# Expert products dealt to the column tiles anew, and their rows turned by VectorE instead of TensorE

## The reference

```
def block_ffn(args):
    xb, e = args
    return (jax.nn.silu(xb @ w_gate[e]) * (xb @ w_up[e])) @ w_down[e]
```

## Time and profile before

| what | value |
|---|---|
| time, median of 3 runs | 1782.14 us |
| lowest and highest | 1778.94 and 1787.34 us |
| profiled execution | span 1782.2 us, the only time that its page gives |
| PE busy, PEld busy | 1547.8 us (87%), 1104.7 us (62%) |
| DVE, ACT, POOL busy | 977.4 us (55%), 649.6 us (36%), 180.4 us (10%) |
| DMA | 305.70 MB, mean 172 GB/s |
| hidden products L2647, 4992 matmuls | 309.3 us busy |
| down products L2663, 2464 matmuls | 147.3 us busy |
| transposes L2655, 77 | mean 334 ns each |

### The profile page before, as it was taken

One profiled execution on the slowest core, in us unless ns is written; L12 is line 12 of the kernel. 1 busy time (PEld: TensorE's weight loads), 2 busy tenths in 40 slices (PEclk: granted clock), 3 DMA queues, 4 the chain that ended last, 5 costly groups with the idle time before them and its releaser, 6 DMA issues. The chain is left out here.

```text
span 1782.2 us, 47179 instructions
## 1 busy us (share of the span) xinstructions
PE 1547.8 (87%) x19513; PEld 1104.7 (62%) x19513; DVE 977.4 (55%) x1789; ACT 649.6 (36%) x1646; POOL 180.4 (10%) x261
## 2 busy tenths in 40 slices
PE   5799989999978898879989788739999999996758
PEld 3588876789767888746666677625555555543323
DVE  5797743331045665569998466660404435455637
ACT  4544421112345455346667445312222222221110
POOL 0000100000045543200000000000000000000021
PEclk8899998999969999989999999859999999999879
DMA  9322315540233443130110244276467579999967
GB/s 350 118 71 90 115 45 206 177 162 7 89 116 109 127 129 97 51 127 19 42 48 7 87 154 154 80 257 244 157 225 273 199 291 370 385 396 398 382 209 299
DMA packets 150760, 305.70 MB, mean 172 GB/s; under 512 B 10670, under 2 KB 53118, under 8 KB 147202
## 3 DMA queue, kind: packets, MB, share of 16 engines
q1 hardware_dynamic: 128674, 245.33, 38.2%
q0 software_dynamic: 10336, 46.67, 7.4%
q10 hardware_dynamic: 11520, 10.49, 1.9%
HBM read 256.79 MB, written 45.66 MB: 170 GB/s over the span
## 5 line engine op out<-in xcount | busy, mean ns | idle before, releaser
L2647 PE MATMUL psum<-now_hidden,i_xm 128*32 128x256 f32 x4992 | 309.3, 389 | 28.1 <-DVE now_hidden L2753 26.3
L2647 PEld LDWEIGHTS psum<-now_hidden,i_xm 128*32 128x32 f32 x4992 | 150.3, 111 | 150.3 <-DVE now_hidden L2753 33.3
L2663 PE MATMUL psum<-now_down,i_hT 128*32 128x256 f32 x2464 | 147.3, 379 | 14.2 <-DVE now_down L2752 14.2
L2753 DVE COPY now_hidden<-raw_hidden 128x1024 f32 (+1 forms) x176 | 109.2, 692 | 78.4 <-DMA raw_hidden<-in_w_up 38.1
L2765 DVE TENSOR_TENSOR i_h<-i_silu,psum 128x128 f32<-128x128 f32 x78 | 22.2, 284 | 215.5 <-ACT i_silu L2702 215.5
L2663 PEld LDWEIGHTS psum<-now_down,i_hT 128*32 128x32 f32 x2464 | 78.8, 110 | 70.5 <-DVE now_down L2752 19.9
L1906 PE MATMUL psum<-dkT,f_qT 64*128 64x512 f32 (+1 forms) x384 | 91.2, 581 | 23.6 <-ACT f_E L1957 21.1
L2752 DVE TENSOR_TENSOR now_down<-raw_down,rep_g 128x1024 f32<-128x1024 f32 x88 | 101.8, 1218 | 8.7 <-PE psum L2663 8.7
L121 PE MATMUL psum<-hT_head,wm_head 128*128 128x512 f32 (+1 forms) x256 | 96.8, 378 | 11.2 <-DVE hT_rest L410 6.9
L1957 ACT ACTIVATE f_E<-psum,f_mx 128x1280 f32<-128x1280 f32 (+2 forms) x96 | 92.2, 968 | 16.3 <-DVE f_mx L2016 16.1
L121 PE MATMUL psum<-hT_head,wm_rest 128*128 128x512 f32 (+1 forms) x256 | 95.3, 372 | 0.0
(11 more groups left out here) (362 smaller groups left out, 3019.7 us busy)
## 6 DMA issues: line engine op xcount, KB each, us to landing
raw_hidden<-in_w_gate SPq DMA_DIRECT2D x22, 2048.0 KB, 15.5
raw_hidden<-in_w_up SPq DMA_DIRECT2D x22, 2048.0 KB, 17.1
raw_down<-in_w_down SPq DMA_DIRECT2D x22, 2048.0 KB, 11.8
wa_late<-in_w_ada POOLq DMA_DIRECT2D x16, 1024.0 KB, 6.6
yb<-i_y ACTq DMA_DIRECT2D x80, 128.0 KB
wa<-in_w_ada SPq DMA_DIRECT2D x8, 1024.0 KB, 13.7
wt<-in_w_in SPq DMA_DIRECT2D x4, 2048.0 KB, 8.4
wm<-in_w_in SPq DMA_DIRECT2D x12, 512.0 KB, 3.8
```

The costliest lines, as they stand in the source:

```text
L2647: last = nc.tensor.matmul(hidden_bank(s)[j * SUB:(j + 1) * SUB, :], xm[u][:, k, s * SUB:(s + 1) * SUB], now["hidden"][:, :, k, j * P:(j + ...
L2663: last = nc.tensor.matmul(down_bank(s)[j * SUB:(j + 1) * SUB, :], hT[s % 2][:, k * SUB:(k + 1) * SUB], now["down"][:, k, j * WIDE:(j + 1) ...
L2753: return nc.vector.tensor_copy(now[n][:, :, k, :], src)
```

## The change

The gate and up columns are dealt to the four column tiles in another way: tile j takes columns b*128 + j*32 + x for b in 0 to 3 and x in 0 to 31, where it took j*128 to j*128+127. The moving operand of a hidden product then has 8 runs of 32 columns where it had 2 runs of 128. After `mix`, block (j, b) of 32x32 in `hh` holds 32 tokens by hidden columns b*128 + j*32 and on. Turning each such block where it stands gives the same `hT` as before: chunk b, partitions 32j to 32j+31. VectorE does this with one block transpose from `hh` to `hT`, right behind the product, with a wait for that product and one for the down products that last read this `hT`. `turn_h` on TensorE and `keep_h` on ScalarE are gone, and `down` waits for VectorE's transpose. `down` also waits for the output copy of the block before the last, where it waited for that of the last.

```diff
+    def by_blocks(ap):
+        return ap.rearrange("p (w b x) -> p w b x", w=2, x=SUB)
+    def columns_of(ap, j):
+        return ap.rearrange("p w (b j x) -> p j w b x", j=SUBS, x=SUB)[:, j]
...
-                        last = nc.tensor.matmul(hidden_bank(s)[j * SUB:(j + 1) * SUB, :], xm[u][:, k, s * SUB:(s + 1) * SUB],
-                                                now["hidden"][:, :, k, j * P:(j + 1) * P], start=(k == 0), stop=(k == KD - 1),
+                        last = nc.tensor.matmul(by_blocks(hidden_bank(s)[j * SUB:(j + 1) * SUB, :]), xm[u][:, k, s * SUB:(s + 1) * SUB],
+                                                columns_of(now["hidden"][:, :, k, :], j), start=(k == 0), stop=(k == KD - 1),
                                                 tile_position=(0, j * SUB))
...
-            def turn_h(b, s):
-                pe.wait_ge(mixed, b + 1)
-                pe.wait_ge(h_kept, b)
-                nc.tensor.transpose(m.bank(4, P), hh[s % 2][:, :], ident).then_inc(h_turned, 1)
             def down(b, s, place):
-                pe.wait_ge(h_kept, b + 1)
-                pe.wait_ge(y_kept, b)
+                pe.wait_ge(h_turned, b + 1)
+                if b >= 1:
+                    pe.wait_ge(y_kept, b - 1)
                 pe.wait_ge(copied["down"], place * KE + KE)
...
                 hidden(b + 1, v, r, after, range(KD // 2))
-                turn_h(b, s)
                 hidden(b + 1, v, r, after, range(KD // 2, KD))
                 down(b, s, here)
...
-            def keep_h(b, s):
-                act.wait_ge(h_turned, b + 1)
-                nc.scalar.activation(hT[s % 2][:, :], m.bank(4, P), ACT.Copy).then_inc(h_kept, 1)
...
             def mix(b, s):
                 dve.wait_ge(silued, b + 1)
                 nc.vector.tensor_tensor(hh[s % 2][:, :], hs[:, :], hidden_bank(s)[:, P:2 * P], ALU.mult).then_inc(mixed, 1)
+                dve.wait_ge(mixed, b + 1)
+                if b >= 2:
+                    dve.wait_ge(used["down"], (b - 1) * KE)
+                nc.vector.transpose(hT[s % 2][:, :], hh[s % 2][:, :]).then_inc(h_turned, 1)
```

More of the change, by code:

```diff
@@ L2564, in experts @@
     x_kept = [m.sem(f"i_x_kept{u}") for u in U2]
-    silued, mixed, h_turned, h_kept, y_kept = (m.sem("i_" + n) for n in ("silued", "mixed", "h_turned", "h_kept", "y_kept"))
+    silued, mixed, h_turned, y_kept = (m.sem("i_" + n) for n in ("silued", "mixed", "h_turned", "y_kept"))
     ybt = d["yb"].rearrange("(q s p) (j n) -> q j p s n", s=SUBS, p=SUB, j=SUBS)
@@ L2715, in body @@
                 b = q * SUBS + s
-                keep_h(b, s)
                 if X_PARTS[s][0] < X_PARTS[s][1]:
```

## The result

The changed kernel takes 1793.25 us (median of 10 runs, 1788.90 to 1797.45), beside 1783.22 us for the kernel before on the same chip (10 runs, 1777.91 to 1789.12): a ratio of 1.0058, interval 1.0041 to 1.0074. It is slower by about 10 us where I forecast 22 us less. A time in a trace is that of one profiled execution: span 1795.6 us after, 1782.2 before. The profiled execution of the changed kernel is the slowest of its ten, so the traces differ by somewhat more than the medians.

The account below looks back on a forecast made before the run. TensorE was taken to bound the experts stage up to 1460 us, expert weight loading after it. Savings of 19.1 + 2 + 1.3 = 22.4 us from 1782.1 gave 1759.7, say 1760 us; range 1750 to 1774, 8 times in 10.

Parts of the forecast that it names:

- the chain: At an exchange of experts, from the lone block's hidden products to its down products, VectorE the bound: 0.36 us longer.
- the three swaps: Paired exchanges of expert weights at 1275, 1348 and 1411 us: each loses three bodies' saving and 0.36 us.
- 3 x 0.36 = 1.1: Cost in us of the block transpose at three exchanges of experts, subtracted from 32 bodies' saving of 20.2 us.
- the border: Load issued at 1460.15 us, where the limit passes from TensorE to expert weight loads; to come 19.1 us earlier.
- A plain body: One pass of TensorE's loop without a change of expert: to save 0.63 us, taking some 5.1 instead of 5.7.
- the 0.39: Bound on a body's saving if the new join of the hidden products' halves costs all three waits' price: 0.73 - 0.34.
- The seam: Join between the hidden products' two halves: some 0.1 us stays; rival keeping a gap like that between bodies, 1774 us, chance 0.12.
- The short runs: Hidden products reading 8 runs of 32 columns: claimed to cost 0; rival that they slow every product, 1810 us, chance 0.07.
- 0.067 us spare for a group: Hidden products: four loads and products take 0.174 us, their columns 0.107 at 2.4 GHz, leaving room for short runs.
- The limit of the second half: After 1460 us expert weight loading binds, TensorE's savings worth nearly nothing; rival of a less bound half, 1749 to 1753 us, 0.08.
- 2 + 1.3: Gains in us after 1460 us: 2 from filled dips in the loads, 1.3 behind the last landing.

Follow-up runs that it names:

- `wait_only`: Kernel before, plus only VectorE's wait for its own product and one column of zeros written behind it; ratio 1.0133, 1808.1 us.
- `turn_other`: Changed kernel, but VectorE transposes a constant tile and so needn't wait for its product; ratio 0.9926, 1770.9 us.
- `loads_twice`: Changed kernel with three more VectorE register loads at the head of each body; ratio 1.0205, 1814.6 us.
- `late_turn`: Changed kernel, transpose and its wait behind the scaled down-weight copies, two of VectorE's three places carried over, one register load ahead of the wait; 0.9928, 1769.3 us.
- `late_turn_pe`: As `late_turn`, with TensorE also carrying one of its two places over in a register; ratio 0.9909, 1766.6 us.
- `before_pe`: Kernel before, with only TensorE carrying one of its two places over in a register; ratio 0.9960, 1776.4 us.
- `no_turn`: Changed kernel without any transpose or its waits, the down products reading the unturned product; ratio 0.9904, 1767.7 us.

## Why the prediction was wrong

- **The step that failed is the wait behind the product**: "Queued behind it are only the next copies", and from it "the first block transpose lies between the first product and the scaled copies and makes the chain 0.36 us longer". I counted what VectorE executes and not what its queue does ahead of it. Behind the product stood also branches, register arithmetic and three register loads (0.30 us and 0.19 of arithmetic each), which had been free only because the queue could run ahead. The chain grew by 3.37 us (2.75 at the hidden copies, 0.62 at the scaled ones), not by 0.36. In my sum the three swaps cost "3 x 0.36 = 1.1" and the saving of their bodies; measured, they take 17.5 us more than before. `wait_only`, `turn_other` and `loads_twice` show the cause from three sides. In `turn_other`, without the wait, the same three swaps take only 1.6 us more.
- **It grew once more through the clock.** I had said that TensorE's waits at a swap grow from 1.6 to about 3.3 us; they are 4.09. Behind such a wait the granted clock in the trace is 0.65 over 7.7 us, and weight loads come in fours every 0.43 us, as in the earlier trace rows: the lower level, 1.2 GHz. That step takes 1.99 us more. At 2.57 us (`turn_other`) and 2.59 (`late_turn`) it stays at the full level. From the stage's first swap to the border the changed kernel spends 17.0 us at the lower level (around 1285, 1364 and 1425 us), the kernel before, `turn_other` and `late_turn` none. An estimate says that the clock alone is enough for the 1.99: the lower level lasts from 1286.54 to 1291.9, 5.4 us or 12.6 groups of products at 0.43 us, which take 2.7 at the full level; of the 2.7 lost, 0.6 is a wait that `turn_other` has at that place.
- **A plain body** saved 0.40 us, not 0.63; I had the 0.39 as a bound. The seam indeed has no gap left. What I mis-sized is the pace: I took the distance of weight loads, 43.5 ns, for that of the work. Loads run ahead of products, and products start in groups of four, one for each column tile, every 0.216 us; the four starts of a group are 7 to 11 ns apart, so the 21.8 ns that I read as a pace of issue is only a mean. The trace before shows it: the last group ahead of the transpose starts at 1258.60 us and the first behind it at 1259.20, so 0.59 - 0.216 = 0.38 us was to be had. The 1.64 us of the down products' loads, which I read as the price of three waits, is this pace too (7 x 0.216 and the last load's 0.11 make 1.62). The floor is 24 groups a body, 5.18 us in `late_turn_pe`, or 0.216 us a group, which is 518 cycles of 2.4 GHz for 256 columns. Before, 5.71 - 5.18 = 0.53 us could go at most. The 0.13 us left in the changed body are TensorE's own register loads, which `before_pe` shows with 5.71 to 5.58.
- **The short runs** cost nothing, as said, though for a wrong reason. The two rows four loads apart in the earlier trace rows are one group at 1.2 GHz and not two, so there was no "0.067 us spare for a group". The time went to the side of this rival by another mechanism.
- **The limit of the second half** was read rightly. Without the wait (`turn_other`), the load of the border comes at 1449.0 us, 11.2 us earlier, and the next phase's first gather (1722.26 before) 14.5 us earlier: 3.3 us are gained behind the border, where I had 2 + 1.3. That they agree to the tenth is luck. My own sum with 0.40 in place of 0.63 is 32 x 0.40 - 1.1 + 3.3 = 15.0, or 1767 us: what `turn_other` (1771), `no_turn` (1768) and `late_turn` (1769) show. The forecast of 1760 thus had two faults, 7 us of pace and some 25 us of stalls.
- **Behind the border** the changed kernel also loses. From the border to the next phase's first gather it takes 269.7 us where it took 262.1, and 258.8 in `turn_other`. The swaps stall there too, and the copies that free the raw buffers come late. The DMA engines then have gaps: over the first 41 us behind the border their share is 0.91 (335 GB/s) in the changed kernel and in `wait_only`, 0.96 (347) before and 1.00 (366) in `turn_other`, whose row is this:

```profile
1449.00:1490.00 41.00, 38.57 (x676) 22.57 (x668) 26.56 (x45) 8.58 (x25) 1.88 (x2) 1.00 1.00 366
```

So a stall on TensorE and VectorE was not free in the half that the loads bound, since the same copies free the buffers that the loads need. I had allowed for gains there, never for a loss. Against `turn_other`, the stalls cost 16 us before the border and 11 behind it in these two executions (23.5 by the medians).

Not tried: the late transpose with all three register loads, and the carried places with the transpose at its first position; which of the two carries `late_turn` is open. Nor is it known why the first register load behind the wait took 0.65 us at the swap shown and 0.32 in `loads_twice`.

## What to carry to other kernels

Before an engine is given a wait for its own last instruction, look at what its *queue* does in that time: branches, register loads and waits further on are hidden only as long as the queue can run ahead, and it could not run past any unmet wait that was looked at here. Put such a wait behind the work that others wait for, with the bookkeeping ahead of it, and look at places where that engine is the bound and not at the plain body. A pace is read from starts of groups of products, not from weight loads, which run ahead.

## What the runs showed of the hardware

- An unmet wait holds VectorE's instruction queue, be it for the engine's own product (branch at 1272.85, product's end at 1272.80) or for ScalarE (register loads from 1261.7 on, the awaited start at 1261.51). The three register loads behind it, each a load of 0.30 us and register arithmetic of 0.19, with branches and waits, made 3.2 us bare.
- A float32 product of 256 columns in each of four column tiles starts every 0.216 us for the group of four at 2.4 GHz and every 0.43 at 1.2 GHz, the four within 25 ns of each other. Eight runs of 128 bytes in the moving operand, for two of 512, change nothing (1.0000, 0.9979 to 1.0021).
- VectorE's transpose of 128x128 float32 in 32x32 blocks took 311 to 314 ns in all 78 instances.
- TensorE's waits of 3.62, 3.92, 4.09 and 4.26 us in the rows here were each followed, in `wait_only` 1.5 us later, by weight loads in fours every 0.43 us, the low clock. Those of 2.57 and 2.59 us were not, nor was one of 3.34 us in `loads_twice`, while one of 2.73 us in `late_turn_pe` was, and of two of 4.09 and 4.08 us in the changed kernel the one at 1286.54 us was and the one at 1597.67 us was not: the length of one wait doesn't settle it.
